# Delta-rule chunks of a hybrid decoder layer: the interleaved gate matmuls spread over both halves of every level instead of standing in lumps at the chunk's head and tail

## The reference

```python
gates = jax.nn.sigmoid(gate.reshape(B, L, N_BRANCH, D_MODEL))      # gate = columns of u @ w_in
h = x + jnp.einsum('bld,de->ble', jnp.sum(gates * br, axis=2), w_o)
```

```python
m = jnp.where(strict, jnp.einsum('nbhid,nbhjd->nbhij', kc, kc) * decay * bc[..., :, None], 0.0)
a = m + jnp.eye(C, dtype=F32)
sol = lax.linalg.triangular_solve(a, rhs, left_side=True, lower=True, unit_diagonal=True)
...
w = u_c - jnp.einsum('bhck,bhkv->bhcv', kcum_c, s)
o = jnp.einsum('bhck,bhkv->bhcv', qd, s) + jnp.einsum('bhij,bhjv->bhiv', qk_c, w)
s = s * gt + jnp.einsum('bhck,bhcv->bhkv', kd, w)
```

## Time and profile before

| | |
|---|---|
| median of 3 runs | 3167.27 us (3166.82 to 3168.12) |
| the profiled execution, its own time | 3168.18 us |
| its span, first to last instruction | 3166.0 us |
| PE busy | 2870.8 us, 91% of the span |
| VectorE / ScalarE / GpSimd busy | 46% / 40% / 26% |
| mean granted TensorE clock | 0.92 of full speed |

### The profile page before, as it was taken

The page is one execution under the profiler, slowest core; times in us unless marked ns, Lnnn a source line. Parts: engine busy times, 40 slices in busy tenths (PEclk is TensorE's granted clock), DMA queues, the critical chain, the costliest instruction groups (busy, mean ns, idle before and its releaser), DMA issues. The chain is left out here.

```text
span 3166.0 us, 56495 instructions
## 1 busy us (share of the span) xinstructions
PE 2870.8 (91%) x22382; PEld 2692.5 (85%) x22382; DVE 1461.3 (46%) x2218; ACT 1268.4 (40%) x2305; POOL 813.9 (26%) x364
## 2 busy tenths in 40 slices
PE   4998999989996989999879989899899879899996
PEld 3998988888886979999868989788788779899995
DVE  2362764654423526346035448456544243561641
ACT  3431434762213335345244224457422152552542
POOL 1221221220000424444222213122200034244441
PEclk7998899999976989999979979999999589899997
DMA  5222334534323513232232222254333344223321
GB/s 168 74 76 63 98 102 131 152 118 118 108 71 101 188 54 82 84 96 76 73 98 82 65 81 91 81 176 155 108 105 95 93 130 144 56 68 100 94 83 53
DMA packets 366308, 315.83 MB, mean 100 GB/s; under 512 B 42710, under 2 KB 314488, under 8 KB 365494
## 3 DMA queue, kind: packets, MB, share of 16 engines
q10 hardware_dynamic: 257332, 188.09, 20.0%
q1 hardware_dynamic: 108706, 124.05, 13.3%
HBM read 273.70 MB, written 38.38 MB: 99 GB/s over the span
## 5 line engine op out<-in xcount | busy, mean ns | idle before, releaser
L768 POOL TENSOR_TENSOR w_lo<-w_raw,w_hi 128x1024 fp32r<-128x1024 f32 (+2 forms) x360 | 813.7, 2261 | 2294.2 <-ACT w_hi L1370 2294.1
L775 PE MATMUL big<-uhi,w_hi 128*128 128x272 f32 x3968 | 1197.4, 302 | 53.9 <-DVE ulo L1876 24.4
L777 PE MATMUL big<-uhi,w_lo 128*128 128x272 f32 x3968 | 1160.9, 293 | 0.0
L776 PE MATMUL big<-ulo,w_hi 128*128 128x272 f32 x3968 | 1155.3, 291 | 0.0
L775 PEld LDWEIGHTS big<-uhi,w_hi 128*128 128x128 f32 x3968 | 760.6, 192 | 102.1 <-issue 50.6
L776 PEld LDWEIGHTS big<-ulo,w_hi 128*128 128x128 f32 x3968 | 763.5, 192 | 3.7 <-issue 1.9
L777 PEld LDWEIGHTS big<-uhi,w_lo 128*128 128x128 f32 x3968 | 760.5, 192 | 0.0
L1370 ACT ACTIVATE w_hi<-w_raw 128x1024 fp32r<-128x1024 f32 (+2 forms) x360 | 343.7, 955 | 346.5 <-PE big L777 317.6
L775 PE MATMUL big<-hhi,w_hi 128*128 128x272 f32 x704 | 204.5, 290 | 1.4 <-DVE hlo L2402 1.4
L777 PE MATMUL big<-hhi,w_lo 128*128 128x272 f32 x704 | 203.2, 289 | 0.0
L776 PE MATMUL big<-hlo,w_hi 128*128 128x272 f32 x704 | 202.4, 287 | 0.0
(11 more groups left out here) (350 smaller groups left out, 4104.9 us busy)
## 6 DMA issues: line engine op xcount, KB each, us to landing
w_raw<-in_w_in ACTq DMA_DIRECT2D x66, 1024.0 KB, 5.7
w_raw<-in_w_up ACTq DMA_DIRECT2D x88, 512.0 KB, 5.1
kpage<-in_cache_k SPq DMA_DIRECT2D x128, 256.0 KB, 3.0
w_raw<-in_w_down ACTq DMA_DIRECT2D x32, 704.0 KB, 4.7
d_conv<-in_cache_v SPq DMA_DIRECT2D x64, 256.0 KB, 2.7
d_pad<-in_cache_v SPq DMA_DIRECT2D x64, 256.0 KB, 2.7
gate_dram<-gate_raw ACTq DMA_DIRECT2D x48, 272.0 KB, 2.3
sig<-gate_dram SPq DMA_DIRECT2D x48, 272.0 KB, 3.4
```

The costliest lines, as they stand in the source:

```text
L768: po.tensor_tensor(split_view(lo, t), tile_of(t), split_view(hi, t).bitcast(F32), ALU.subtract).then_inc(w_lo.sem, w_lo.next(t))
L775: pe.matmul(out, wh, xh, start=start, stop=False)
L776: pe.matmul(out, wh, xl, start=False, stop=False)
L777: return pe.matmul(out, wl, xh, start=False, stop=stop)
```

## The change

The 32 gate steps of a prompt chunk are divided anew over the same PE program. Nothing else is computed, and no step is added or taken away.

| place on PE | steps before | steps after |
|---|---|---|
| head, ahead of `dkT` | 10 | 4 |
| head, between `dkT` and Y1 | 2 | 0 |
| each of six levels, after `level_y(li, 0)` and its page | 0 | 2 |
| each of six levels, after `level_y(li, 1)` and its page | 2 | 2 |
| after the last `level_t` | 3 | 2 |
| between `kc` and `dw` | 5 | 2 |

The first tile's 16th step falls in level 4 before and in level 8 after. On ScalarE `store_gate` of that tile moves from behind the copy of Y(8, 0) to behind the copy of Y(8, 1).

```diff
             if c < 4:
                 value_page(next(pages))
                 value_page(next(pages))
-                advance(gates, 10)
+                advance(gates, 4)
             turn(X[0], ('dkT', c), P, n, [k[:, h, :] for h in range(H)], P)
-            if c < 4:
-                advance(gates, 2)
             pe.wait_ge(vec_out.sem, vec_out.at(('first', c)))
...
                 level_y(li, 0)
                 if c < 4:
                     value_page(next(pages))
+                    advance(gates, 2)
                 if li > 1:
                     level_t(li - 1, 1)
...
             level_t(len(levels) - 1, 1)
             if c < 4:
-                advance(gates, 3)
+                advance(gates, 2)
...
             if c < 4:
-                advance(gates, 5)
+                advance(gates, 2)
             pe.wait_ge(X[1].drained, X[1].at(('kc', c)))
...
-                    if c < 4 and s == LEVELS[3] and hp == 0:
+                    if c < 4 and s == LEVELS[3] and hp == 1:
                         store_gate(*DELTA_GATES[2 * c], 1)
```

## The result

The changed kernel takes 3177.5 us (median of 7 runs, 3173.51 to 3179.88), beside 3166.82 us before (7 runs, 3163.58 to 3168.12) on the same chip. The ratio is 1.0035, with an interval from 1.0023 to 1.0046: slower, by 7.3 to 14.6 us. The forecast was 3176.0 us. The profiled execution took 3177.5 us, its span is 3175.3; against the profiled 3168.18 and 3166.0 that is 9.3 us more.

A forecast was written before the change was run, and what follows sets the result against it. PE, busy 91% of the span, was taken as the bound. A chunk: 0.04 + 1.01 + 0.16 - 0.24 + 0.12 = +1.09 us; eight chunks, +8.7 on the median of 3167.27, give 3176.0 us, range 3170.5 to 3180.5.

The forecast's parts named there:

- Tail, `dw`: Between `kc` and `dw`: with two steps left, `dw` waits 1.01 us a chunk, plus a restart of 0.08.
- the two terms of `kc`: Tail, ahead of `kc`: one step less gives a wait of 0.04 us and a restart of up to 0.08.
- Head free: Chunk head: 12 steps become 4 at no cost; Y1 has 1.25 us to spare, the page two us.
- level 2 a gain: First half of level 2: two steps cover `level_t`'s wait for ScalarE's copy of Y, gaining 0.24 us a chunk.
- Levels 4 to 64 neutral: Added steps stand outside the waits at `level_y(li, 1)`: nothing gained or lost; a level grows by its 0.76 us of steps.
- the rival of the shrinking level waits: Steps remove some 1.5 us a chunk of level waits; kernel 3164 us if wholly; chance 0.14 for part or whole.
- Store of the first tile: Level 8 onward: the moved store adds short waits on PE, 0.12 us a chunk, between 0 and 0.25.
- The clock: Tail: nothing charged; the clock should stay 1.00 in the prompt chunks despite a wait of 1.1 us.
- The rival with the low clock in the tail: Clock falls to 0.50 in the tail once a chunk: +16 us more, kernel 3192; chance 0.04.

The follow-up runs named there:

- e1: Kernel before with three of the five gate steps between `kc` and `dw` moved, one each, into the first halves of levels 16, 32 and 64; 3178.72 us.
- e10: Kernel before with each step pair of levels 4 to 64 moved from behind the second page to ahead of `level_y(li, 1)`; 3157.19 us.
- e5: Kernel before with two gate steps moved from the head, ahead of `dkT`, to the first half of level 2; 3164.52 us.
- e9: Kernel before with the pair of gate steps between `dkT` and Y1 moved behind Y1; 3164.11 us.
- e4: Kernel before with only the first tile's store moved on ScalarE, from behind the first Y copy of level 8 to the second; 3174.22 us.

## Why the prediction was right, and what it lacked

**Tail, `dw`: right.** Forecast was a start 2.64 behind `kc` and 1.09 us with the restart. Measured is 2.72 behind a `kc` that itself restarted (1.13 for its eight matmuls in place of 1.05), in all eight chunks. Of the two terms of `kc`, the wait of 0.04 measured 0.09 (1.28 behind the last `level_t`, where 1.57 less a step is 1.19), and the restart of 0.08 measured 0.08, in its length. e1 shows the tail alone at 1.1 us a chunk.

**Head free, level 2 a gain: right.** The rows of the changed kernel, second chunk, for the earlier trace rows:

```profile
767.19 1.44 SPq L727 DMA_DIRECT2D d_conv<-in_cache_v  x2
767.83 0.69 DVE L2234 TENSOR_TENSOR d_T<-consts,d_lm 128x512 f32<-128x512 f32 x1
...
769.33 0.60 PE L837 MATMUL aux<-consts,qkv 128*128 128x128 f32 x4
...
769.77 0.60 PE L837 MATMUL aux<-consts,d_T 128*128 128x128 f32 x4
...
771.21 0.68 PE L1200 MATMUL aux<-d_T,d_lm 128*128 128x128 f32 x4 [0.84 <-ACT d_T L1369]
...
771.82 0.42 PE L1143 MATMUL big<-d_conv,s_pT 128*32 128x128 f32 x8
...
773.03 0.38 PE L1212 MATMUL aux<-d_y,d_T 128*128 128x128 f32 x2
```

`d_T` is ready at 768.52, and Y1 starts 1.25 later: the spare time that the prediction has, to the hundredth. The page's buffer, reloaded from 767.19 on, is wanted at 771.82, and 2.7 after the issue is 769.9. Behind the page stand two steps, and `level_t` shows no wait.

**Levels 4 to 64 neutral: right.** The second Y of level 4 still follows VectorE's update by 0.10 (778.59 + 0.69 = 779.28, Y at 779.38), and level 64 keeps its idle of 0.45:

```profile
778.59 0.69 DVE L2198 TENSOR_TENSOR d_T<-d_T,aux 128x512 f32<-128x512 f32 x1 [3.71 <-PE aux L1214]
...
779.38 0.68 PE L1200 MATMUL aux<-d_T,d_lm 128*128 128x128 f32 x4
...
802.21 0.68 PE L1200 MATMUL aux<-d_T,d_lm 128*128 128x128 f32 x4 [0.45 <-issue]
```

This is why the rival of the shrinking level waits fell. e10 shows what it would have been worth, 1.42 us a chunk, with the same two steps put a few instructions later.

**Store of the first tile: its own wait right, its follower missed.** The page that precedes the next tile's first step is at 787.26 and the step at 787.77, 0.51 where 0.36 is usual: 0.15 us, beside the 0.12 of the sum.

```profile
787.00 0.62 ACT L1369 ACTIVATE gate_raw<-big 128x544 f32<-128x544 f32 x1 [0.94 <-PE big L777]
...
787.26 0.43 PE L1143 MATMUL big<-d_pad,s_pT 128*32 128x128 f32 x8
...
787.77 0.36 PE L775 MATMUL big<-uhi,w_hi 128*128 128x272 f32 x1
```

What failed is the end of that paragraph of the prediction: it followed the store through ScalarE to the copy of Y and stopped. Behind ScalarE's `w_hi` hangs GpSimd's `w_lo`, which I did not move in my working though it moves with the store. Through it the store costs another 0.57 us in six chunks, 3.4 us in all. The rows that would have warned are of before: there `w_lo` takes 2.50 us beside the mask product, where elsewhere it takes 2.35, and begins 0.42 behind the start of that product. The rows of a layer's last chunk, shown with e5 and e9 above, would have warned louder: there the two begin at the same time.

```profile
783.79 0.69 DVE L2188 TENSOR_TENSOR d_lm<-d_mt,consts 128x512 f32<-128x512 f32 x1
...
784.21 2.50 POOL L768 TENSOR_TENSOR w_lo<-w_raw,w_hi 128x1024 fp32r<-128x1024 f32 x1 [21.41 <-ACT w_hi L1370]
```

The Trainium skill, "SBUF — State Buffer", section "Who interferes with whom", states that a VectorE instruction with two SBUF inputs contends with a GpSimd instruction that reads SBUF, while one with at most one SBUF input, outside its two-port modes, does not; that the shared ports are an exclusive lock; and that the order of issue decides which of the two is blocked. The traces agree: the mask product (two SBUF inputs) went from 0.69 to 1.58, the update (one input from PSUM) stayed at 0.69 beside the same `w_lo`, and with the product ahead in before it was `w_lo` that got longer, by 0.15 and, in a layer's last chunk, by 0.57. The prediction did not apply this to the move of the store.

**The clock: right.** The rival with the low clock in the tail would have given 3192; the stretch from 808 to 858 in the changed kernel has a granted clock of 1.00, the higher of the two levels, as the earlier trace rows has it. So have its stretches 757 to 907 and 2306 to 2455.

```profile
808.00:858.00 50.00, 47.93 (x452) 41.77 (x452) 21.64 (x36) 11.43 (x22) 4.72 (x2) 1.00 0.35 107
```

**The total: nearer than its terms, by luck.** With the true terms, eight chunks of 1.13 and six times 0.57, the sum is 12.5 us, while the profiled pair differs by 9.3. The forecast had 8.7: it lacked 3.4 us for the mask products, and some 3 us of the 12.5 came back outside the prompt chunks, which it did not forecast either. The range would have held without that luck, but barely: 3167.27 and 12.5 is 3179.8. The starts of the sample chunk's `kc` are 6.16 apart in the first layer (of before, then of after); up to there the layer's loss, by its terms four chunks of 1.13 and three times 0.57, is still nearly whole:

```profile
921.40 1.88 PE L1239 MATMUL aux<-d_T,d_kb 32*128 32x32 f32 x8 [0.46 <-DVE d_T L2199]
```

```profile
927.56 1.29 PE L1238 MATMUL aux<-d_T,d_kb 32*128 32x32 f32 x8 [0.46 <-DVE d_T L2198]
```

Those of the second phase's first matmuls (2256.72 and 2260.67) are only 3.95 apart. The stretches between, which hold the same work, are 1335.30 us before and 1333.10 after:

```profile
921.40:2256.70 1335.30, 1217.35 (x9251) 1158.54 (x9252) 633.81 (x939) 571.68 (x1026) 390.12 (x172) 0.92 0.33 98
```

```profile
927.60:2260.70 1333.10, 1215.00 (x9252) 1157.03 (x9252) 634.00 (x939) 571.30 (x1026) 390.11 (x172) 0.92 0.33 98
```

The `kc` above is part of it: 1.88 us before and 1.29 after. The granted clock was 0.50 between 921 and 923 before, and 1.00 between 925 and 927 and 0.80 between 927 and 929 after. That such stretches move when everything ahead of them comes later was in the prediction, as 2 us to either side. How much of the 3 us belongs to the change, and how much to these two executions, stays open: the runs of one kernel spread over 4 to 10 us. For all eleven kernels the sum from the chunks lies inside the interval of its ratio, so nothing larger is hidden outside the chunks.

## What to carry to other kernels

Filler work is worth only what it covers: look for the two ends of each wait (the last instruction that feeds it, and the one that waits) and put it between them. A few instructions to the left or right it is worth nothing, as e10 and the changed kernel show with the same steps. Steps that stand between such ends already are not spare, however lumped they look; compare the time from producer to consumer with the other engines' chain before taking one away (here 2.77 against 2.64). And when a store or copy moves, follow everything that it releases, engine by engine to the last, and lay each against what runs there now.

## What the hardware showed that I had not expected

A GpSimd subtraction and a VectorE product, both with two operands in SBUF, don't run side by side: the one that comes second takes longer. The product takes 1.58 to 1.82 us in place of 0.69 and ends 0.54 to 0.56 behind the subtraction, in all 18 cases of these runs (792.07 behind 791.52, 889.17 behind 888.62, and so on). That is less than its own 0.69, so some 0.14 of it was done or overlapped.

That one figure fits the other cases too, by the rows shown above. The second one gets longer by the time for which it overlaps the first, less 0.12 to 0.14: `w_lo` by 0.15 at an overlap of 0.27, `w_lo` by 0.57 at 0.69, the product by 0.89 at 1.03 and by 1.11 at 1.25. In e4 the overlap was 0.07 (791.00 to 791.07), below that figure, and the product kept its 0.69. This is an estimate from these rows; why the first 0.12 to 0.14 is free, no row shows.

A head start of 0.02 us for the subtraction was enough. At 0.01 or less the rows don't tell which goes first: with both at 881.45 in the kernel before it was the product, with both at 2426.06 in e5 the subtraction.
